# Key stage of a hybrid decoder step: prompt compression interleaved with the first sample's keys, compressed scores computed per sample, first score units moved behind the loop

## The chip, the cores and the metric

The program runs on one core of one Trainium2 chip. The metric is the device time of one execution in microseconds (us); lower is better. The engines' names in the profile: PE is TensorE (PEld its weight loads), DVE is VectorE, ACT is ScalarE, POOL is GpSimd, SP is SyncE, which in this kernel only issues transfers.

## The reference, cut to what matters

One layer of a decoder for 512 prompt tokens and 8 samples with 2048 past tokens each. Two groups of heads share one input projection: stick-breaking attention (`sb`, 8 heads) and NSA (8 query heads on 2 key heads) with a compressed, a selected and a window branch. For the samples, keys and values lie in caches by pages of 128 tokens (16 pages for each sample). The part that the change touches computes for every sample:

```python
z = einsum('bqhd,bshd->bhqs', q, k) / sqrt(64)            # stick-breaking scores of all 2048 cached keys
kc = silu((blocks_k + pe_k) @ w_ck1) @ w_ck2               # compressed keys: blocks of 32 tokens, stride 16
vc = silu((blocks_v + pe_v) @ w_cv1) @ w_cv2               # the same for values: 127 blocks a sample, 31 for the prompt
s_c = einsum('bkgqd,bkcd->bkgqc', qg, kc) * scale          # compressed scores
s_s = einsum('bkgqd,bkqnld->bkgqnl', qg, kg) * scale       # scores of the selected pages; the window's likewise
```

`pe @ w1` is the same for all blocks; the kernel adds it as a bias (`pebias`), for one column per hidden unit.

## The kernel before, in words

Each engine has a program of its own, written out by hand; semaphores order them. There is no scheduler: what stands in a row in the code of an engine is issued in that row, and an instruction that waits holds up all behind it on its engine. The stages in order of time: norm and input projection (to about 182 us), transposes of queries and keys (182 to 189), the key stage (189 to 454), the two attention stages for the prompt with the samples' small steps and value pages among them, the output projection and the MLP.

**Ahead of the loop of the key stage (before).** PE multiplies `pe` by `w1`, one column at a time (two times 16 products, lines 745 to 750), DVE copies the two columns to `pebias` (L1729, L1730). Then `compress(0, 1, ...)` compresses the prompt's own keys and values: PE transposes (`chunks_T`, L780), multiplies by `w1` (`hidden`, L794: four groups of 8 products, two for keys, two for values), ACT copies the transposes (L1308) and makes the sigmoid (`sigmoid`, L1312), DVE finishes the silu (`silu`, L1734, L1742), PE multiplies by `w2`. POOL reorders tokens ahead of each (`permute`, L2202, L2205). All else of the key stage waits until this is done.

**The loop (before).** Four turns of two samples. For one sample:
- SP (`load_keys`, L525) issues 50 transfers: the sample's stick-breaking query row (L529), 2 times 8 pieces of the *next* sample's tokens to be compressed (`load_chunks`, L495, L498), the selection keys in quads of 4 pages (L540), 16 pages of stick-breaking keys into a ring of 8 slots (L543), the window keys as a fifth quad (L546). A quad waits until PE has transposed the quad two before it, a ring slot until DVE has reduced the page before it in the slot. Page numbers come by a table load (L491), four times a sample.
- PE (`compress(c, 2, between)`, L774) does the same work as for the prompt with 127 blocks. In six places it calls `between()`, which takes the next piece of key work: `keys_T` (L756, four transposes of a quad, waits for the quad) or `key_scores` (L765). Pieces: T0; S0 and T1; S1 and T2; S2 and T3; S3 and T4; S4. Pieces five and six stand ahead of the `w2` products.
- DVE takes pages of the ring (`sb_keys`, L1752: a product L1760, a sum L1764): 8 pages, the silu of the keys, 6 pages, the silu of the values, 2 pages, two copies (`compressed_out`, L1745).

**Behind the loop (before).** All compressed scores (8 small products), the gates (one product), ACT rounds five constant masks to fp32r (L1370, L1374; the last two wait for the compressed scores), takes a softplus over 1024 columns (L1378, L1379) and only then the first unit of the stick-breaking stage, `sb_ln(0)` (L1387 to L1389). PE issues `sb_qk(0)`, the first unit's scores, behind the gates. DVE prepares the samples' scores (L1984 to L1996), waits for the transposed row maxima (`row_max_diagonal`, L1816, L1817) and then takes `sb_soft(0)` (L2006). A unit of this stage runs PE, ACT, DVE, ACT, DVE, PE, ACT in a chain.

## Time and profile before

| | us |
|---|---|
| median of 3 runs | 1187.35 (1182.03 to 1191.99) |
| the profiled execution | 1191.54 |
| its span | 1189.7 |
| mean granted TensorE clock | 0.929 of full |
| PE busy | 1084.4 (91%) |
| DVE, ACT, POOL busy | 617.1, 392.6, 69.9 |

The profile is of one execution, whose time was 1191.54 us, 4.2 us above the median of the runs; 1.8 us of it lie outside its span. Times in the timeline are us from the span's start. A row of the timeline merges instructions of one kind that follow each other; fp32 products show as two instructions each, so a `key_scores` of 4 products is 8 in the rows. PE's busy time counts a product from its start to its modelled end, whatever the clock; the granted clock stands in rows of its own (1.00 is 2.4 GHz, 0.50 is 1.2 GHz).

### The profile page before, as it was taken

The numbers are of one execution on the slowest core, as the hardware profiler recorded it, in microseconds if no ns is written. First come the engines' busy times: TensorE is split into PE (matmuls) and PEld (weight loads), VectorE is DVE, ScalarE is ACT, GpSimd is POOL, SyncE is SP. The second block draws the span as 40 slices with busy tenths as digits, with TensorE's granted clock in tenths as the row PEclk, the third lists the DMA queues.
The fourth block names the chain that finished last, engine by engine and source line by source line (L and its number), as shares of the span: only waits on it lengthen the run. The fifth ranks groups of instructions, "written<-read, shape, count | busy, mean of one in ns | idle before, by whom it ended". The sixth has DMA issues, their size and how long they took to land.

```text
span 1189.7 us, 23077 instructions
## 1 busy us (share of the span) xinstructions
PE 1084.4 (91%) x8348; PEld 953.0 (80%) x8348; DVE 617.1 (52%) x1042; ACT 392.6 (33%) x725; POOL 69.9 (6%) x83
## 2 busy tenths in 40 slices
PE   3996999998989998989999898999999999999993
PEld 2996999887878886555555557999999999999993
DVE  4431673586778787765444436445543335553332
ACT  4120212333333335556444435332231112221223
POOL 2000001221112100000000000110000000000002
PEclk9998997798999896988999978999999999999997
DMA  7529218799999963256666651323333333332321
GB/s 248 178 79 222 79 40 230 188 241 246 268 265 275 273 209 115 90 187 202 212 200 205 212 177 36 89 71 88 88 106 89 94 85 89 94 97 72 90 71 72
DMA packets 180131, 177.61 MB, mean 149 GB/s; under 512 B 13063, under 2 KB 140676, under 8 KB 177700
## 3 DMA queue, kind: packets, MB, share of 16 engines
q1 hardware_dynamic: 178610, 171.33, 50.7%
q10 hardware_dynamic: 1458, 5.43, 1.4%
q8 instruction: 40, 0.66, 0.2%
q14 instruction: 23, 0.19, 0.1%
HBM read 170.83 MB, written 10.06 MB: 152 GB/s over the span
## 4 chain that ended last, share of the span: by engine, by line
PE 64%; SPq 18%; issue 6%; DMA 4%; DVE 3%; ACT 3%; POOL 0%; POOLq 0%; DVEq 0%; ACTq 0%
PE bank L662 59%; SPq L576 4%; PE bank L666 4%; SPq L498 3%; SPq L540 2%; SPq L564 2%; SPq L543 2%; SPq L491 2%; DMA low_arena<-in_cache_nsa_slc_kv_dram 1%; DMA low_arena<-in_consts_dram 1%; DMA high_arena<-in_cache_sb_kv_dram 1%; DMA high_arena<-in_w_in_dram 1%; ACT low_arena L1550 1%; SPq L504 0%; SPq L582 0%
## 5 line engine op out<-in xcount | busy, mean ns | idle before, releaser
L662 PE MATMUL bank<-high_arena 128*128 128x254 f32 (+8 forms) x1864 | 239.6, 346 | 16.5 <-DMA high_arena<-in_cache_sb_kv_dram 6.6
L662 PEld LDWEIGHTS bank<-high_arena 128*128 128x128 f32 (+5 forms) x1864 | 185.2, 152 | 53.6 <-issue 10.1
L2114 DVE TENSOR_TENSOR w_low<-high_arena,w_high 128x1024 fp32r<-128x1024 f32 x72 | 90.1, 1252 | 84.1 <-ACT w_high L1487 74.2
L666 PE MATMUL bank<-low_arena 128*128 128x128 f32 (+3 forms) x658 | 108.0, 309 | 28.0 <-DMA page_ids<-in_page_table_dram 14.7
L666 PEld LDWEIGHTS bank<-low_arena 128*128 128x128 f32 (+3 forms) x658 | 87.4, 164 | 39.6 <-issue 27.2
L1487 ACT ACTIVATE w_high<-high_arena 128x1024 fp32r<-128x1024 f32 x72 | 76.3, 1060 | 114.8 <-PE bank L662 113.8
L662 PE MATMUL bank<-a_high,w_high 128*128 128x256 f32 (+1 forms) x512 | 104.3, 285 | 5.3 <-issue 2.9
L662 PE MATMUL bank<-h_high,w_high 128*128 128x256 f32 (+1 forms) x512 | 103.1, 283 | 1.8 <-DVE h_low L2141 1.8
L662 PE MATMUL bank<-a_low,w_high 128*128 128x256 f32 (+1 forms) x512 | 103.8, 284 | 0.0
L662 PE MATMUL bank<-a_high,w_low 128*128 128x256 f32 (+1 forms) x512 | 103.5, 283 | 0.0
L662 PE MATMUL bank<-h_low,w_high 128*128 128x256 f32 (+1 forms) x512 | 103.3, 283 | 0.0
L662 PE MATMUL bank<-h_high,w_low 128*128 128x256 f32 (+1 forms) x512 | 103.2, 283 | 0.0
L1764 DVE TENSOR_REDUCE low_arena<-low_arena 128x512 f32 x128 | 87.9, 686 | 18.3 <-DVE low_arena L1760 0.6
L662 PE MATMUL bank<-w_in_high,h_high 128*128 128x284 f32 x320 | 96.1, 300 | 0.8 <-issue 0.8
L662 PE MATMUL bank<-w_in_low,h_high 128*128 128x284 f32 x320 | 94.7, 296 | 0.0
L662 PE MATMUL bank<-w_in_high,h_low_in 128*128 128x284 f32 x320 | 94.6, 296 | 0.0
L1760 DVE TENSOR_TENSOR low_arena<-low_arena,high_arena 128x512 f32<-128x512 f32 x120 | 86.1, 718 | 12.0 <-DMA low_arena<-in_cache_sb_kv_dram 11.9
L662 PEld LDWEIGHTS bank<-a_high,w_high 128*128 128x128 f32 x512 | 80.0, 190 | 6.1 <-issue 5.9
L662 PEld LDWEIGHTS bank<-h_high,w_high 128*128 128x128 f32 x512 | 79.4, 188 | 2.0 <-issue 2.0
L662 PEld LDWEIGHTS bank<-a_high,w_low 128*128 128x128 f32 x512 | 80.0, 190 | 0.0
L662 PEld LDWEIGHTS bank<-a_low,w_high 128*128 128x128 f32 x512 | 79.9, 189 | 0.0
L662 PEld LDWEIGHTS bank<-h_high,w_low 128*128 128x128 f32 x512 | 79.6, 189 | 0.0
(218 smaller groups left out, 1583.6 us busy)
## 6 DMA issues: line engine op xcount, KB each, us to landing
low_arena<-in_cache_sb_kv_dram SPq DMA_DIRECT2D x128, 256.0 KB, 4.9
high_arena<-in_cache_sb_kv_dram SPq DMA_DIRECT2D x128, 256.0 KB, 3.7
high_arena<-in_cache_nsa_cmp_kv_dram SPq DMA_DIRECT2D x128, 128.0 KB, 5.2
high_arena<-in_w_up_dram SPq DMA_DIRECT2D x32, 512.0 KB, 4.1
high_arena<-in_w_down_dram SPq DMA_DIRECT2D x32, 512.0 KB, 4.2
high_arena<-in_w_in_dram SPq DMA_DIRECT2D x10, 1136.0 KB, 5.6
low_arena<-in_cache_nsa_slc_kv_dram SPq DMA_DIRECT2D x128, 64.0 KB
high_arena<-in_cache_nsa_slc_kv_dram SPq DMA_DIRECT2D x128, 64.0 KB, 2.4
```

The lines of the kernel that those rows point to most:

```text
L491: return nc.values_load_multi_w_load_instructions(pt[0:1, ds(lo, 8)], engines=[mybir.EngineType.SP], min_val=0, max_val=NPHYS - 1, skip_ru ...
L498: sp.dma_start(nat[u][half][16 * p:16 * p + 16].rearrange("p t k h d -> p (t k h d)"), c_cmp[ds(pg, 1)].rearrange("o (c t) k h d -> (o c) ...
L540: sp.dma_start(kquad[n % 2][:, j], c_slc[ds(pages[p + j], 1), :, 0].rearrange("o s h d -> (o s) (h d)")).then_inc(sem(f"kq_in{n % 2}"), 16)
L543: sp.dma_start(kring[p], c_sb[ds(pages[p], 1), :, 0].rearrange("o s h d -> (o s) (h d)")).then_inc(sem(f"ring_in{p}"), 16)
L564: sp.dma_start(ring[:, u, :], c_sb[ds(pages[u], 1), :, 1].rearrange("o s h d -> (o s) (h d)")).then_inc(sem(f"ring_in{u}"), 16)
L576: sp.dma_start(quad[:, q, j, :], c_slc[ds(pages[4 * (q % 2) + j], 1), :, 1].rearrange("o s h d -> (o s) (h d)")).then_inc(sem(f"quad_in{q} ...
L662: return T.matmul(out, lhsT=l, rhs=r, start=start, stop=stop, **k)
L666: return T.transpose(out, in_, ident[0:n, 0:n])
L1487: S.activation(w_hi_r[u], w_raw[u], ACT.Copy).then_inc(sem(f"w_hi{u}"), 1)
L1760: chain(V.tensor_tensor(k, k, qb[:, u, :], ALU.mult))
L1764: V.tensor_reduce(raw_scores(ds(i, 1), u)[:, p, :], k.rearrange("p (h d) -> p h d", h=H), AX.X, ALU.add).then_inc(sem(f"ring_free{p % 8}"), 1)
L2114: V.tensor_tensor(w_lo_r[u], w_raw[u], w_hi[u], ALU.subtract).then_inc(sem(f"w_lo{u}"), 1)
```

## The change

1. **Loads.** The compression tokens of sample 1 are loaded behind the last weight block of the input projection, in place of in the key stage (`load_keys(0, 0, False)`). SP no longer waits for `snew` ahead of all key loads, only ahead of ring slot 7. The buffers `nat[1]`, and that of the prompt's tokens, lie elsewhere.
2. **Bias.** The 32 one-column products go. The prompt's `hidden` takes 66 columns for 62: two more per key head, of which one comes out as `pe @ w1`. DVE copies it from there (`bias`).
3. **Front.** Three pieces of sample 0's key work (T0; S0 and T1; S1 and T2) stand inside the prompt's `compress`, and DVE takes pages 0 to 6 of sample 0 among the prompt's silus. Samples 0 and 1 are written out, the loop has three turns.
4. **Compressed scores.** Each sample's 8 columns are computed within its `compress`, behind the `w2` product of the keys, and copied by ACT with the other scores (`csc`). DVE copies the compressed keys ahead of the silu of the values. PE's piece five stands behind the keys' `w2` product.
5. **Early.** The gates' product and ACT's rounding of all five masks stand in and behind sample 0.
6. **Behind the loop.** PE issues `sb_qk(0)` and `sb_qk(1)` first; ACT takes `sb_ln(0)` ahead of the softplus.

```diff
@@ SP @@
             load_columns(*COLUMNS[1])
+            sp.wait_ge(sem("z_mm"), 5 * NCB // 2)
+            for half in range(2):
+                load_chunks(page_ids(NPG + 8 * half), 1, half)
...
+                        if p == 7:
+                            sp.wait_ge(sem("snew"), 2)
                         sp.wait_ge(sem(f"ring_free{p}"), i * 4 + 2 * u + half + 1)
...
             sp.wait_ge(sem("sbq_out"), 16)
-            sp.wait_ge(sem("snew"), 2)
-
-            with sp.Fori(0, 3) as i:
+
+            load_keys(0, 0, False)
+            load_keys(0, 1, True)
+            with sp.Fori(1, 3) as i:
                 for u in range(2):
                     load_keys(i, u, True)
@@ PE @@
             pe.wait_ge(sem("cmpw_in"), 64)
-            for kv in range(2):
-                for m in range(16):
-                    ins = mm(bank[6][:, kv:kv + 1], w1[kv][:, m, :], vcol[:, 24 + 16 * kv + m:25 + 16 * kv + m],
-                             m == 0, m == 15)
-            ins.then_inc(sem("start_pe"), 1)
...
+                nh = nb if tiles == 2 else NCP + 2
...
-                        mm(out, w1[kv][:, m, :], xT[kv][:, m, :, 0:nb], m == 0, False)
-                        ins = mm(out, w1[kv][:, 8 + m, :], xT[kv][:, m, :, 1:nb + 1], False, m == 7)
+                        mm(out, w1[kv][:, m, :], xT[kv][:, m, :, 0:nh], m == 0, False)
+                        ins = mm(out, w1[kv][:, 8 + m, :], xT[kv][:, m, :, 1:nh + 1], False, m == 7)
...
                 hidden(1, 1)
-                between()
-                between()
                 pe.wait_ge(sem("hid_ready0"), c + past + 1 + 1)
...
                 ins.then_inc(sem("w2_mm0"), 1)
+                between()
+                if past:
+                    pe.wait_ge(sem("kvc_ev0"), c + past + 1 + 1)
+                    mm(bank[7][0:NC, 160:160 + H], kc[:, 0, 0:NC],
+                       qbd[:, ds(c, 1), :].rearrange("p o j -> p (o j)"))
+                between()
...
-            compress(0, 1, lambda: None)
-            with pe.Fori(0, 4) as i:
+            todo = key_work(0, 0)
+            compress(0, 1, next_of(todo, 3))
+            todo[2:2] = [lambda: None, sample_gates, lambda: None]
+            compress(0, 2, next_of(todo))
+            compress(1, 2, next_of(key_work(0, 1)))
+            with pe.Fori(1, 4) as i:
...
-            sample_scores()
-            sample_gates()
-            pe.wait_ge(sem("masks_in"), 1)
...
+            pe.wait_ge(sem("masks_in"), 1)
+            sb_qk(0)
+            sb_qk(1)
+            for kv in range(2):
+                pe.wait_ge(sem(f"kvc_ev{kv}"), B + 1 + 1)
+            pe.wait_ge(sem("qs_ev"), B + 1)
@@ ACT @@
+            todo = key_copies(0, 0)
+            compress(0, 1, lambda: todo.pop(0)() if len(todo) > 1 else None)
+            sample_keys(0, 0, todo)
+            act.wait_ge(sem("sbq_out"), 16)
+            act.wait_ge(*signal("g_mm", 1))
+            for dst, name in ((ident_r, "ident"), (causal_r, "causal"), (before_r, "before"), (ntri_r, "ntri"), (nones_r, "nones")):
+                ins = S.activation(dst, K(name), ACT.Copy)
+            ins.then_inc(sem("masks_in"), 1)
...
                 if s < SB_U:
                     sb_ln(s)
+                if s == 0:
+                    sample_softplus()
@@ DVE @@
+            def bias(kv):
+                dve.wait_ge(sem(f"hid_mm{kv}"), 1)
+                col = bank[2 + kv][:, NCP + 1:NCP + 2]
+                chain(V.tensor_copy(pebias[:, kv:kv + 1], col))
+                V.tensor_scalar(pebias[:, 2 + kv:3 + kv], col, -1.0, None, ALU.mult).then_inc(sem("start_dve"), 1)
...
+            def sample_work(i, u, begun=0):
+
+                c = i * 2 + u
+                sb_keys(i, u, begun, 8)
+                silu(c, 0, NCH)
+                sb_keys(i, u, 8, 14)
+                keys_compressed(c, kc[:, 0, 0:NC], NCH)
+                silu(c, 1, NCH)
+                sb_keys(i, u, 14, 16)
+                values_compressed(c, vc[0:NC, ds(c, 1), :].rearrange("p o c -> p (o c)"), NCH)
+
+            sb_keys(0, 0, 0, 2)
+            bias(0)
+            sb_keys(0, 0, 2, 4)
             silu(0, 0, NCP + 1)
+            sb_keys(0, 0, 4, 5)
+            bias(1)
+            sb_keys(0, 0, 5, 7)
             silu(0, 1, NCP + 1)
```

PE between the last transpose of the queries and the second group of the prompt's products; a product with 62 or 66 columns is one of `hidden`, 128x64 a transpose of the prompt's tokens, 128x128 with a wait on `kq_in` a key quad (T), 128x8 key scores (S). Before:

```order
L662 MATMUL bank<-low_arena_49,high_arena_50 128x1 [waits cmpw_in]
L662 MATMUL bank<-low_arena_49,high_arena_50 128x1 x31
L666 MATMUL bank<-low_arena_49 128x64 [waits start_dve,perm,qkT_ev0,xT_ev0,qkT_ev1]
L666 MATMUL bank<-low_arena_49 128x64 x3
L666 MATMUL bank<-low_arena_49 128x64 [waits xT_ev0,perm]
L666 MATMUL bank<-low_arena_49 128x64 x3
L662 MATMUL bank<-high_arena_50 128x62 [waits xT_ev0,hid_ready0]
L662 MATMUL bank<-high_arena_50 128x62 x7
```

And now:

```order
L677 MATMUL bank<-low_arena_49 128x64 [waits start_dve,qkT_ev0,perm,qkT_ev1,xT_ev0,cmpw_in]
L677 MATMUL bank<-low_arena_49 128x64 x3
L677 MATMUL bank<-low_arena_49 128x128 [waits kq_ev,kq_in0]
L677 MATMUL bank<-low_arena_49 128x128 x3
L677 MATMUL bank<-low_arena_49 128x64 [waits xT_ev0,perm]
L677 MATMUL bank<-low_arena_49 128x64 x3
L673 MATMUL bank<-high_arena_50 128x66 [waits xT_ev0,hid_ready0]
L673 MATMUL bank<-high_arena_50 128x66 x7
L673 MATMUL bank<-high_arena_50 128x8 [waits qs_ev,kq_ev]
L673 MATMUL bank<-high_arena_50 128x8 x3
L677 MATMUL bank<-low_arena_49 128x128 [waits kq_ev,kq_in1]
```

The one-column products are gone, and the second instruction group of the prompt's compression now stands behind a wait for the first key quad.

DVE at the end of the prompt's compression and in sample 0 now (L1788 and L1792 are a page's product and sum, L1757 and L1758 the bias, L1769 a silu):

```order
L1757 COPY high_arena<-bank 128x1 [waits hid_mm1]
L1758 TENSOR_SCALAR high_arena<-bank 128x1 [waits dve_steps]
L1788 TENSOR_TENSOR low_arena<-low_arena,high_arena 128x512 [waits ring_in5]
L1792 TENSOR_REDUCE low_arena<-low_arena 128x8 [waits dve_steps]
L1788 TENSOR_TENSOR low_arena<-low_arena,high_arena 128x512 [waits ring_in6]
L1792 TENSOR_REDUCE low_arena<-low_arena 128x8 [waits dve_steps]
L1769 SCALAR_TENSOR_TENSOR high_arena<-bank,high_arena 128x2x31 [waits w2_mm1,hid_e1]
L1774 COPY high_arena<-bank 128x31 [waits w2_mm0]
L1778 COPY high_arena<-bank 31x128 [waits w2_mm1]
L1788 TENSOR_TENSOR low_arena<-low_arena,high_arena 128x512 [waits ring_in7]
L1792 TENSOR_REDUCE low_arena<-low_arena 128x8 [waits dve_steps]
L1769 SCALAR_TENSOR_TENSOR high_arena<-bank,high_arena 128x2x127 [waits w2_mm0,hid_e0]
```

Two pages stand between the values' bias and the values' silu of the prompt, and page 8 still stands behind the keys' silu of sample 0 (the last row).

PE behind the loop, before (`before_r,ident_r` is the mask product of a unit; 127x8 the compressed scores):

```order
L662 MATMUL bank<-high_arena_50 127x8 [waits qs_ev,kvc_ev1,kvc_ev0]
L662 MATMUL bank<-high_arena_50 127x8 x7
L662 MATMUL bank<-high_arena_50,low_arena_49 128x192 [waits rows_in]
L662 MATMUL bank<-low_arena_49 128x128 [waits masks_in]
L662 MATMUL bank<-low_arena_49 128x128
L662 MATMUL bank<-before_r_64,ident_r_60 128x128 x2
L666 MATMUL bank<-low_arena_49 64x128 [waits samples_dve]
L662 MATMUL bank<-low_arena_49 128x256 x2
```

And now:

```order
L673 MATMUL bank<-low_arena_49 128x128 [waits masks_in]
L673 MATMUL bank<-low_arena_49 128x128
L673 MATMUL bank<-before_r_64,ident_r_60 128x128 x2
L673 MATMUL bank<-low_arena_49 128x256 x2
L673 MATMUL bank<-before_r_64,ident_r_60 128x128 x2
L677 MATMUL bank<-low_arena_49 64x128 [waits qs_ev,samples_dve,kvc_ev1,kvc_ev0]
```

Two units' scores come first; the transpose of the row maxima (64x128) stands behind them.

## Rows read from the trace of the kernel before

**Rows 1.** The page, part 2: busy and clock in 40 slices of 29.7 us.
```profile
PE   3996999998989998989999898999999999999993
...
PEclk9998997798999896988999978999999999999997
```
**Rows 2.** Busy time by stretch, one per sample: us, PE, PEld, DVE, ACT, POOL, clock, DMA, GB/s.
```profile
369.46:396.00 26.54, 25.52 (x167) 23.21 (x166) 22.79 (x38) 10.17 (x21) 6.01 (x8) 0.98 1.02 261
...
sum 234.90, PE 217.37 PEld 196.66 DVE 179.75 ACT 82.98 POOL 39.15; mean PE 27.17 PEld 24.58 DVE 22.47 ACT 10.37 POOL 4.89
```
**Rows 3.** What SP's queue waited for, 185 to 460 us: total, times, longest.
```profile
SPq L540 <- PE bank L666: 16.1, 8, 6.9
...
SPq L551 <- DVE high_arena L1721: 4.3, 1, 4.3
```
**Rows 4.** Timeline of SP's queue, start us and us: query rows, first chunks, ring loads.
```profile
194.12 0.37 SPq L529 DMA_DIRECT2D high_arena<-sb_queries  x1
195.46 4.03 SPq L498 DMA_DIRECT2D high_arena<-in_cache_nsa_cmp_kv_dram  x8
...
235.30 0.34 SPq L529 DMA_DIRECT2D high_arena<-sb_queries  x1
...
249.37 1.88 SPq L543 DMA_DIRECT2D low_arena<-in_cache_sb_kv_dram  x4
...
414.12 0.43 SPq L529 DMA_DIRECT2D high_arena<-sb_queries  x1
```
**Rows 5.** Busy time by stretches of 2 us (columns as in rows 2).
```profile
190.00:192.00 2.00, 2.00 (x20) 2.00 (x20) 1.90 (x4) 1.59 (x2) 2.00 (x4) 1.00 1.04 426
...
216.00:218.00 2.00, 1.71 (x11) 1.46 (x10) 0.00 (x0) 0.58 (x2) 0.00 (x0) 0.50 0.96 148
```
**Rows 6.** The query rows' transfers (L529), from issue to landing.
```profile
DMA to landing us min/median/max: 4.6/6.6/8.2
```
**Rows 7.** Timeline of PE, 188 to 245 us.
```profile
189.39 9.94 PE L662 MATMUL bank<-low_arena,high_arena 128*128 128x1 f32 x64
...
206.04 3.67 PE L662 MATMUL bank<-high_arena 128*128 128x62 f32 x16
...
218.73 0.64 PE L662 MATMUL bank<-high_arena 128*31 128x64 f32 x4 [1.02 <-DVE high_arena L1742]
219.30 3.68 PE L666 MATMUL bank<-low_arena 128*128 128x128 f32 x16
...
229.16 3.59 PE L662 MATMUL bank<-high_arena 128*128 128x254 f32 x16
...
240.10 4.38 PE L662 MATMUL bank<-high_arena 128*128 128x254 f32 x24
```
**Rows 8.** Timeline of DVE: the prompt's last silu, then sample 0.
```profile
218.40 0.28 DVE L1742 SCALAR_TENSOR_TENSOR high_arena<-bank,high_arena 128x62 f32<-128x62 f32 x1 [7.16 <-ACT high_arena L1319]
...
234.28 0.48 DVE L1742 SCALAR_TENSOR_TENSOR high_arena<-bank,high_arena 128x254 f32<-128x254 f32 x1 [2.57 <-ACT high_arena L1319]
234.68 0.68 DVE L1760 TENSOR_TENSOR low_arena<-low_arena,high_arena 128x512 f32<-128x512 f32 x1
...
236.11 0.82 DVE L1760 TENSOR_TENSOR low_arena<-low_arena,high_arena 128x512 f32<-128x512 f32 x1
...
245.22 0.48 DVE L1742 SCALAR_TENSOR_TENSOR high_arena<-bank,high_arena 128x254 f32<-128x254 f32 x1 [1.34 <-ACT high_arena L1319]
```
**Rows 9.** Timeline behind the loop: PE, ACT, DVE.
```profile
455.01 3.55 PE L662 MATMUL bank<-high_arena 128*127 128x8 f32 x16 [0.84 <-DVE high_arena L1748]
...
459.16 0.39 DVE L1996 COPY high_arena<-high_arena 64x31 f32<-64x31 f32 x2
...
461.09 0.28 DVE L1816 TENSOR_REDUCE low_arena<-bank 64x1 f32<-64x128 f32 x1 [1.55 <-PE bank L666]
461.14 0.36 ACT L1387 ACTIVATE high_arena<-bank 128x256 f32<-128x256 f32 x1
...
462.53 0.42 DVE L2006 SCALAR_TENSOR_TENSOR high_arena<-bank,high_arena 128x256 f32<-128x256 f32 x1 [0.87 <-ACT high_arena L1389]
```

More of the change, by code:

```diff
@@ L194, with __init__ @@
 class Turns:
-    def __init__(self, chain, count, per):
-        self.chain, self.count, self.per = chain, count, per
+    def __init__(self, chain, count, per, start=0):
+        self.chain, self.count, self.per, self.start = chain, count, per, start
     def __enter__(self):
@@ L202, in __enter__ @@
         self.first = c.n
-        self.loop = c.eng.Fori(0, self.count)
+        c.n = self.base = c.n - self.start * self.per
+        self.loop = c.eng.Fori(self.start, self.start + self.count)
         i = self.loop.__enter__()
@@ L1696, in _ @@
             V.memset(st[0:1, 204:205], 0.0).then_inc(sem("start_dve"), 1)
+            for kv in range(2):
+                ins = V.tensor_copy(xT[kv][:, :, :, NCP + 1:NCP + 3],
+                                    over(vcol[:, 24 + 16 * kv:40 + 16 * kv].rearrange("p (two m) -> p m two", two=2), 2, KVH))
+            ins.then_inc(sem("start_dve"), 1)
             for j in range(0, 14, 2):
```

162 lines of the change are left out of this document (75 added, 87 removed).

## The prediction

> **What bounds the kernel now.** I read the page's slices first: PE is busy nearly all of the span and its clock is granted in full, but for a few slices; two of the low ones are the seventh and eighth, 178 to 238 us, where the key stage begins [rows 1]. The change works there and up to the end of that stage, so I then cut the stage by sample. The eight samples take 234.9 us. The cheapest is the sixth with 26.5 us at a clock of 0.98, while the mean is 29.4, so PE's own work is not the whole price [rows 2]. SP's queue tells the rest: in the whole stage it waited 16.1 us for PE in 8 places, the longest 6.9, and by the timeline these lie before 235 and behind 414; between its query rows at 235.30 and 414.12 it issues without a pause, 178.8 us for six samples or 29.8 each [rows 3, 4]. From sample 1 on the stage goes at SP's pace. So a change of the front pays only as far as it brings SP sooner to its unbroken run, and behind the loop only as far as it brings the first stick-breaking unit sooner.
>
> **Part 1: where SP stands.** SP's wait for `snew` ended at 194.1 after 4.3 us; without it SP starts at 189.8 [rows 3, 4]. Without 16 chunk transfers (two groups like that of 4.03 us) and their page numbers it also has some 10 us less to issue. Taken alone that is 14 us (I come back to it as a rival). The chunks go where SP and the transfer engines have room, behind the last weight block: cost nothing; if they held up that block, PE would wait by up to their 8 us, but they stand behind it in the same queue.
>
> The run starts, however, when ring slots come free, and these come from DVE, which waits for PE. So I follow that loop.
>
> *First key quad.* Query row at 189.8, page numbers as before 1.34 us (194.12 to 195.46), then four transfers of 0.5 us: the last goes out at 192.6 [rows 4]. The engines have just then finished the prompt's stores: their share is 1.04 at 190 to 192 [rows 5]. A landing takes 4.6 to 8.2 us for 256 KB, as much as a quad; the queue is empty, so 4.6: 197.2 [rows 6]. Bounds: 3 us sooner or 3.6 later.
>
> The Trainium skill, DMA: Bandwidth & Descriptors, on the anatomy of one DMA, gives about 2.0 us of fixed cost and the bytes on top. By it the quad would land 1 to 2 us sooner and the time would be as much lower. No row shows a landing under 4.6 for this size, so it gives the forecast nothing.
>
> *The prompt's compression.* The one-column products filled 189.39 to 199.33 [rows 7]; they go, 9.9 us. But now PE stands from about 191.5 to 197.2 in front of the quad. From there its work until the values' `hidden` is done, at the price of the half clock, goes by its kinds of groups. H, eight products, 3.67 (206.04; 66 columns for 62 cost at most 0.2 more each), four times: 14.7. T, four transposes, 3.68/4 = 0.92, three times: 2.8. S, four key scores, half of the 3.55 of the eight compressed scores, 1.78, twice: 3.6. Two small transposes of the prompt, 0.6 each: 1.2 [rows 7, 9]. Sum 22.3; with 0.5 for hand-overs it ends at 220.0 (before 217.7, as ACT's sigmoid and DVE's silu ended at 218.7). The first half, which ends the keys' `hidden`, is 12.2: 209.4. Then DVE: bias 0.2, two pages of 1.43 (234.68 to 236.11), 2.9, and as before 0.9 from the silu to PE's first transpose of sample 0 (218.40 to 219.30) [rows 7, 8]. Sample 0 starts at 224.0: **4.7 later** than now.
>
> Why the half clock: before, from 194 on, one-column and 62-column products ran at 0.50, and still did at 216 to 218 with PE busy 1.71 of 2 us [rows 5]. The new front has the same products and an idle stretch in front of them.
>
> *Sample 0.* To the end of the keys' `hidden` PE had T0; S0, T1 beside the rest and took 13.4 us (219.3 to 232.7). Now it has S2, T3; S3, T4: one S more at half clock, +1.8. So DVE's silu, before at 234.28, comes 4.7 + 1.8 = 6.5 later and page 8, which stands behind it, starts at 241.2 for 234.68. Six pages 8.6 and the silu 0.4, then pages 14 and 15, 2.9: slot 7 is free at 253.1 (the values' `hidden` has three pieces fewer and is done in time) [rows 7, 8]. SP's load into slot 7 was issued last of the four of 249.37, at 250.8, and nothing held it but SP [rows 4]. **+2.3 us** for the start of SP's unbroken run, and the 29.8 us per sample behind it stay: all that is issued is the same. Bounds: the rivals below, -9 and +6.
>
> **Part 2: in the loop.** One compressed score of 0.2 (3.55/8 at half clock is 0.44; at full clock half) per sample is added, and the keys' `w2` product of 0.3 moves into a place where PE waited 0.8 for ACT's copy of the last quad. DVE's copy of 0.3 ahead of the values' silu falls into its idle 1.34 [rows 8]. ACT copies 0.2 more. Under SP's pace all of it is hidden; for the last sample, which goes at PE's pace, -0.3 at best: I take **-0.2**, bounds -0.5 and +0.5 each for the one or two samples at PE's pace. The five mask copies, 1.0 us on ACT once between samples 0 and 1, may cost 0.5; DVE, not PE, is last there, so 0. The gates' product, 1 us, lies in sample 0 before the values' `hidden`, which has slack: 0.
>
> **Part 3: behind the loop.** Eight scores (3.55) and the gates (1.0) go from PE's path, the masks and the softplus (2.2) from ACT's. ACT could start the first unit 5.5 us sooner than 461.14. But DVE is late next: its preparation ends at 459.5 whatever PE does (459.16 and two copies of 0.2), less the 0.2 copy of the compressed scores. Then, as between 461.09 and 461.7, the diagonal, 0.6: `sb_soft(0)` starts at 460.1 for 462.53 [rows 9]. **-2.4 us**, and from there on the chain of a unit is as it was. What stands ahead of ACT's rounding of the unit, the softplus, waits for DVE until 457.3 and ends at 459.5, in time. Bounds: -1 (softplus or row maxima late) and -4.4 (everything removed pays).
>
> **Sum.** +2.3 - 0.2 - 2.4 = -0.3 us against the profiled execution (1191.54, span 1189.7). That execution is 4.2 above the median of the runs, so I set the sum against the median: 1187.35 - 0.3 = **1187.0**. A measurement of this kernel tells about 1% (12 us) from no change.
>
> **Rivals.**
> 1. *The clock comes up inside the prompt's compression.* For it: with T and S among them PE has denser work from 197 on. Then four H are 7.4 for 14.7, T and S half. The second and third quad become the limit (issued 0.47 us a transfer, landing 201.5 and 207), the values' `hidden` ends at 211, sample 0 starts at 215.4, the silu comes at 229, slot 7 is free at 241.5: -9.3, with the rest -12: **1175**. Against: [rows 5] show 0.50 for work as dense as that, 190s to 220s. The Trainium skill, TensorE: Matmul & The Clock Gate, on the HAM clock gate, says that sustained activity releases the throttle; by that rule a PE that works without a stop from 197 on would get its full clock back there, and this rival would be the case. The trace before does not agree: busy over 0.85 and still 0.50.
> 2. *SP keeps its whole lead.* 14 us and 2.6 behind: **1171**. For it: 14 us are really gone from its queue. Against: slots 0 to 7 wait for pages 8 to 15, and page 8 stands behind a silu that waits for PE.
> 3. *Slower: the key quads land late.* They now stand in PE's path in the prompt's compression, each behind ring loads in the one queue. At the longest landing, 8.2 us [rows 6], the first comes 3.6 later, and the window quad of sample 0, issued only when page 7 has freed its slot (226), lands at 235, when PE wants it. With 1 to 2 us for that, and low clock again behind it: +6 and up: **1193**. It decides from a landing of 6 us on, since PE has no other work ahead of T0.
> 4. *The change doesn't do what it says:* ACT's first unit isn't sooner since DVE's steps hold all. Then part 3 is -0.5, 1189; it lies in the forecast's own range.
>
> **Chances.** Forecast with rival 4, 1182 to 1191: 0.58. Rival 1 in full or in part: 0.20. Rival 2: 0.10. Rival 3: 0.12. The range takes in rival 3 and rival 1: 1173 to 1193. Faster by over 1% (below 1175.5): rival 2 (0.10), most of rival 1 (0.13), and 0.03 of the forecast's case for a stage that gives more than I see: 0.26. Slower by over 1% needs twice the price of rival 3: 0.08. Within 1%: 0.66.
>
> **What would show it right or wrong.** In the new trace: PE idle from about 191.5 to 197 in front of a key transpose; granted clock 0.50 to beyond 220; the prompt's last silu near 223 and sample 0's first transposes near 224; page 8 near 241; SP pausing some 6 us in front of the first ring load of sample 1, and then six samples of 29.8 us. The loop's end some 2 us later than 454.2, and `sb_soft(0)` 5.9 us behind the last `w2` product for 8.4 now. The forecast is wrong if the clock is 1.00 between 200 and 215, if page 8 starts before 235, or if the samples behind the front take less than 29 us each.

## The result, and the profile after

The changed kernel takes 1196.25 us in the median of 20 runs (1184.91 to 1206.91), the kernel before 1185.28 in 20 (1178.09 to 1195.18): a ratio of 1.0092, with a 95% interval of 1.0066 to 1.0118. It is some 11 us slower, where 1187.0 and "no change" had been forecast. The profiled execution took 1196.56 us (span 1194.7). The interval leaves out 1.000, so the loss is real, though smaller than the scatter of single runs. The ratios, here and below, leave out runs over 1.5% above the fastest of their kernel: two of the 20 here, and four of the twelve of e1 below, whose median over all twelve is 1.0097 of that of the kernel before.

The page's slices, which answer to [rows 1]:

```profile
PE   3997997898978998888998988999999999999993
...
PEclk9998996698888888799999898999999999999996
```

The seventh and eighth slice have 6 for 7, and slices 10 to 15, in the loop, have 8 six times, where four of them had 9 before. By sample (columns as in [rows 2]):

```profile
220.04:249.72 29.68, 26.89 (x141) 23.57 (x141) 12.18 (x21) 8.71 (x19) 4.85 (x8) 0.87 0.60 143
...
311.33:339.76 28.43, 27.77 (x167) 25.20 (x168) 22.18 (x36) 10.42 (x21) 5.41 (x8) 0.91 0.89 234
339.76:376.09 36.33, 27.08 (x168) 24.28 (x168) 23.20 (x37) 10.55 (x24) 5.62 (x8) 0.91 1.07 235
...
406.82:441.82 35.00, 30.91 (x169) 27.44 (x168) 23.55 (x38) 10.91 (x25) 5.56 (x8) 0.82 0.85 233
...
sum 249.96, PE 224.82 PEld 200.97 DVE 172.32 ACT 83.63 POOL 37.54; mean PE 28.10 PEld 25.12 DVE 21.54 ACT 10.45 POOL 4.69
```

The eight samples take 249.96 us for 234.90. The fifth alone takes 36.33, of which PE is busy 27.08: it stood for 9. PE is busy 7.5 us more over all, at a lower clock. So the stage from sample 0 on lost 15 us, and the forecast had -0.2 in the loop. The fifth and the seventh sample of the kernel before, for comparison:

```profile
338.68:369.46 30.78, 26.69 (x167) 24.07 (x166) 22.30 (x37) 10.38 (x21) 5.59 (x8) 0.94 1.06 272
...
396.00:426.44 30.44, 27.75 (x165) 25.04 (x166) 22.62 (x37) 10.48 (x21) 5.48 (x8) 0.89 0.95 265
```

Comparing moments needs one care. What lies ahead of the key stage scatters by some us from execution to execution (the prompt's first store goes out at 175.00 us here, at 178.27 in the trace before, and between 174.97 and 181.70 in the eighteen kernels tried below), so I count from that store, and call it S. Four places carry the ledger:

| | before | after | difference |
|---|---|---|---|
| sample 0's first transposes, behind S | 41.0 | 45.0 | +4.0 |
| SP loads sample 1's second page into slot 7, behind S | 72.7 | 76.2 | +3.5 |
| DVE's last copy of compressed values, behind S | 276.4 | 295.7 | +19.3 |
| from there to `sb_soft(0)` | 7.90 | 5.73 | -2.2 |

The front and the end are about as forecast; between the second row and the third 15.8 us are lost. At `sb_soft(0)` the changed kernel is 17.1 us behind; at the end of the span it is 8.3 behind, counted from S. Between 520 and 720 us, in stages whose code is the same, the granted clock was 0.97 for 0.88 in the trace before, which gives back most of that; it is one execution against one, and I read nothing of the change into it.

What did SP do in the loop? The chain of waits of the changed kernel at the end of sample 3, followed back through SP (start us, us, what):

```profile
330.23 0.45 SPq L556
330.67 0.04 issue
330.72 0.04 SPq L564
330.75 0.04 issue
330.80 0.05 SPq L564
330.85 3.92 issue
334.77 0.04 SPq L564
```

L564 is the end of `with sp.Fori(1, 3)`: a register is counted up, a branch is taken at 330.80, and the next instruction comes 3.92 us later. "issue" means that SP waited for nothing that the profile shows. The same place of the kernel before:

```profile
326.15 0.45 SPq L546
326.59 0.04 issue
326.64 0.03 SPq L553
326.67 0.04 issue
326.71 0.04 SPq L553
326.76 0.23 issue
326.98 0.04 SPq L553
```

There the branch cost 0.23 us (and 0.27 at 265.9, where the loop turned the first time). What the gap does, 5 us on, in the timeline of PE and DVE:

```profile
341.28 1.92 SPq L548 DMA_DIRECT2D low_arena<-in_cache_nsa_slc_kv_dram  x4
...
347.24 1.96 PE L677 MATMUL bank<-low_arena 128*128 128x128 f32 x8 [6.43 <-DMA low_arena<-in_cache_nsa_slc_kv_dram]
347.82 0.69 DVE L1788 TENSOR_TENSOR low_arena<-low_arena,high_arena 128x512 f32<-128x512 f32 x1 [6.98 <-DMA low_arena<-in_cache_sb_kv_dram]
```

The quad and the page of the ring are issued late; PE stands 6.43 us for the one and DVE 6.98 us for the other. By SP's query rows sample 3 lasts 35.9 us for 30.2, and 3.7 of these 5.7 us are the gap. From sample 4, the fifth, on PE then works at a lower clock: granted 0.91, 0.89, 0.82 and 0.92 for 0.94, 0.98, 0.89 and 0.93 before. From these figures I estimate some 30 us at half clock for some 15, and PE is busy 113.9 us for 106.9 in these four samples, with the same products but for one compressed score each. That fits a standing which comes back as a slower PE, and in sample 6 SP waits for PE (1.7 us in front of its window quad). It is one trace against one, and no run takes apart how much of the stage's 15.8 us each of these steps carries. SP's longest wait for PE, 5.5 us at 427.1, is another matter: it lies in sample 7, where SP runs ahead of PE in every kernel (3.5 us at the same place before).

The page's third part has the trace of it in one line, the queue that loads instructions (packets, MB, share). Before, and after:

```profile
q14 instruction: 23, 0.19, 0.1%
```
```profile
q14 instruction: 33, 0.27, 0.1%
```

Ten more loads of 8 KB each. Not all of them belong to the gap: the changed kernel with its loop moved (e13 and e17 below) has no gap and still 28 and 29 loads, so that four or five of the ten go with the branch and the rest stay without it. What ties the gap to a load is its time. By the trace's records one begins at 333.15 us, within the gap, and has ended 1.3 us before SP's next instruction; in the kernel before no load lies behind either branch.

### The profile page after: what moved, and what is told of

The parts are those of the page before. It is cut to its first block, busy times and chain, and to the rows that moved or that the text cites. A ratio compares the mean times of both kernels' runs of the same rounds, so it can differ in the third digit from the quotient of the medians.

```text
span 1194.7 us, 22803 instructions
## 1 busy us (share of the span) xinstructions
PE 1071.5 (90%) x8284; PEld 941.7 (79%) x8284; DVE 619.2 (52%) x1045; ACT 394.5 (33%) x733; POOL 69.0 (6%) x83
## 4 chain that ended last, share of the span: by engine, by line
PE 58%; SPq 18%; issue 7%; DVE 7%; DMA 5%; ACT 4%; POOL 0%; ACTq 0%; POOLq 0%; DVEq 0%
PE bank L673 54%; SPq L587 4%; PE bank L677 4%; SPq L503 3%; SPq L548 3%; SPq L553 2%; SPq L575 2%; SPq L496 2%; DMA high_arena<-in_w_in_dram 2%; DMA low_arena<-in_cache_nsa_slc_kv_dram 1%; DMA low_arena<-in_consts_dram 1%; DVE w_in_low L1656 1%; ACT low_arena L1570 1%; DMA high_arena<-in_cache_sb_kv_dram 0%; SPq L509 0%
## 5 line engine op out<-in xcount | busy, mean ns | idle before, releaser
L673 PE MATMUL bank<-high_arena 128*128 128x254 f32 (+8 forms) x1864 | 244.8, 345 | 21.1 <-DMA high_arena<-in_cache_sb_kv_dram 9.9
L673 PEld LDWEIGHTS bank<-high_arena 128*128 128x128 f32 (+4 forms) x1864 | 190.1, 155 | 58.9 <-issue 15.5
L1788 DVE TENSOR_TENSOR low_arena<-low_arena,high_arena 128x512 f32<-128x512 f32 x120 | 86.8, 723 | 22.6 <-DMA low_arena<-in_cache_sb_kv_dram 22.6
L1792 DVE TENSOR_REDUCE low_arena<-low_arena 128x512 f32 (+1 forms) x128 | 87.8, 686 | 14.8 <-DVE low_arena L1788 0.5
```

The costliest lines, as they stand in the source:

```text
L673: return T.matmul(out, lhsT=l, rhs=r, start=start, stop=stop, **k)
L1788: chain(V.tensor_tensor(k, k, qb[:, u, :], ALU.mult))
L1792: V.tensor_reduce(raw_scores(ds(i, 1), u)[:, p, :], k.rearrange("p (h d) -> p h d", h=H), AX.X, ALU.add).then_inc(sem(f"ring_free{p % 8}"), 1)
```

## The experiments

All ratios are to the kernel before, with their 95% intervals.

### SP or the engines?

Four kernels tell "SP's list" (theory A) from "PE's and DVE's order" (theory B).

**e1_wait_once**, the changed kernel with

```
-                        if p == 7:
+                        if p == 7 and half == 0 and isinstance(i, int) and i * 2 + u == 0:
                             sp.wait_ge(sem("snew"), 2)
```

> 

> The changed kernel, but SP's wait for `snew` in front of ring slot 7 is issued for sample 0's first half alone, and no longer twice a sample. Theory A (the key stage goes at the pace of SP's instructions, so that whatever SP gains or loses between two query rows stays in the time): two instructions less per sample, 0.4 us by the query rows (29.69 between 335.04 and 364.73 in the changed kernel, 29.29 for the same sample before), some 2.5 us over seven samples; and the 3.9 us that SP stands behind its loop's branch (330.85 to 334.77) may go or stay, since the loop's code gets shorter by four instructions. Together 2 to 7 us less than the changed kernel, ratio to before 1.003 to 1.008. Theory B (the loss comes from PE and DVE: the compressed score and the copy of the compressed keys stand between PE's products and DVE's pages): no change, 1.009.

Measured 1.0065 (1.0030 to 1.0101), 3.83 us behind the branch. The two instructions take 0.05 us each in SP's row, not 0.4 together. DVE's last copy came 295.8 us behind S for 295.7: the wait carries nothing that can be seen in the trace. The time can't decide it, since the interval reaches from a third of the loss to all of it.

**e2_written_out**, the changed kernel with

```
-            with sp.Fori(1, 3) as i:
+            for i in range(1, 3):
```

> 

> The changed kernel, but SP's loop over samples 2 to 5 is written out, sample by sample, with no branch and with constants for the waits' values. Theory A: the 3.9 us behind the branch go, and a written-out sample costs SP about 28.8 us for 29.7 (as sample 6 before, 28.4 between query rows, for 29.25): 4 x 0.9. In all 7 us less than the changed kernel, ratio to before 1.003; the query rows of samples 2 to 7 are at most 30 us apart and no gap in SP's row is over 1 us without a wait. Theory B: no change, 1.009, since PE and DVE go on at their own pace.

Measured 0.9997 (0.9973 to 1.0021). The loss is gone, with all that the change does to PE, ACT and DVE in place. Query rows of samples 2 to 7 are 28.6 to 29.9 us apart (after: 29.7 to 35.9). This speaks for A and leaves B no room.

**e3_before_written_out**, the same edit in the kernel before, `for i in range(3)`.

> 

> The kernel before, but SP's loop over samples 0 to 5 is written out. Theory A: four or five samples of 28.4 for 29.8 us, 4 to 6 us less: ratio 0.995 to 0.997, the loop ends near 449 for 454.2 behind the same start. Theory B: the same time, 1.000, because SP isn't what bounds. A third reading, that code which runs once must be fetched and costs more than code in a loop: slower, 1.003 and up, with gaps in SP's row at instruction loads.

Measured 0.9998 (0.9968 to 1.0027). Theory A's gain of 4 to 6 us isn't there: the interval allows 3.8 at most. So writing out is worth nothing by itself in a kernel whose branch is cheap; what e2 took away was something that only the changed kernel has.

**e4_scores_behind**, the changed kernel with its compressed scores behind the loop again (in the loop):

```
                 hidden(1, 1)
+                between()
+                between()
...
                 ins.then_inc(sem("w2_mm0"), 1)
-                between()
-                if past:
...
-                between()
```

and DVE's and ACT's copies put back to match.

> 

> The changed kernel with one part undone: the compressed scores are computed behind the loop again, by eight products and a copy of DVE's, and in the loop the keys' `w2` product, DVE's copy of the compressed keys and ACT's copies stand as before; SP's list is untouched. Theory A: in the loop nothing changes, behind it 1 us is lost at most (the products stand behind the first two units' scores): ratio 1.009 to 1.010, and the 3.9 us behind SP's branch are there again. Theory B: the samples go back to 29.4 us, 8 to 12 us less: ratio 0.999 to 1.002.

Measured 1.0102 (1.0063 to 1.0140), 4.58 us behind the branch. Theory B had 0.999 to 1.002: it falls, for what the change does in the loop.

### Is it the branch?

**e6_before_loop_of_two**, the kernel before, nothing of the change in it but the loop's shape:

```
-            with sp.Fori(0, 3) as i:
+            for u in range(2):
+                load_keys(0, u, True)
+            with sp.Fori(1, 3) as i:
                 for u in range(2):
                     load_keys(i, u, True)
```

> 

> The kernel before, with one edit: SP's samples 0 and 1 are written out and its loop runs over turns 1 and 2, as in the changed kernel; what is issued, and in which order, is as before. Theory A1 (a loop of which nothing but this shape has changed has to fetch its first instructions again at its branch): some 4 us between the branch near 327 and the next instruction, and the time 4 to 9 us longer than before: ratio 1.003 to 1.008. Theory A2 (it isn't the shape but something else of the change that makes the branch slow): 0.3 us behind the branch, ratio 1.000.

Measured 1.0067 (1.0031 to 1.0103). The chain of waits of this kernel at its branch:

```profile
323.64 0.05 SPq L555
323.69 4.53 issue
328.22 0.04 SPq L555
```

This is the study's plainest run: the same transfers in the same order, and most of the loss.

**e7_code_shifted**, the changed kernel with 64 superfluous waits in SP's list far ahead (two of them become one instruction, so the loop moves by 32 places and not by the 64 of the expectation):

> 

> The changed kernel with 64 superfluous waits (already met) in SP's list far ahead, behind the norm, in a stretch where SP waits anyway: the loop is the same, but its instructions stand 64 places further on in the program. Theory P (what counts is where the loop's code stands with respect to the blocks of 8 KB in which it is fetched): the gap behind the branch changes, possibly to 0.3 us, and the ratio falls to 1.001 to 1.004. Theory S (the loop is too long for what is kept, wherever it stands): 3.8 to 4.6 us as before, ratio 1.009.

Measured 1.0107 (1.0067 to 1.0148), 4.74 us behind the branch. By itself it spoke for theory S (the loop is too long wherever it stands); it was the wrong shift, as the next kernels show.

**e5_delay_4us** and **e8_written_out_wait_once** are e2 with one thing more each: seven loads of page numbers meant as a delay, and the wait for `snew` issued once.

> 

> The changed kernel with SP's samples written out (as e2, ratio 0.9997), and seven superfluous loads of eight page numbers (0.53 to 0.57 us each, some 4 us) in SP's list in front of sample 4's query row, where the changed kernel stands 3.9 us behind its branch. Theory A (the key stage goes at SP's pace, and the standing behind the branch is the main loss): SP's query rows from sample 4 on come 4 us later and stay so; the next key quad comes 4 us later, PE stands for it some 6 us, the granted clock falls behind that, and the whole run is 4 to 9 us longer than e2: ratio 1.003 to 1.008. Theory C (the standing is absorbed by what lies ready in the ring, and e2 gained by its quicker samples alone): ratio 1.000 as e2.

> 

> The changed kernel with SP's samples written out and the wait for `snew` issued once: the best version that the study has in view. Theory A: two instructions less per sample (0.1 to 0.4 us) than e2, so 1 to 2.5 us less than e2's 0.9997 of before: ratio 0.998. Theory B or C: as e2, 1.000. That it beats the kernel before by more than the interval (0.3%) isn't expected of either.

Measured 1.0028 (1.0000 to 1.0056) and 0.9991 (0.9956 to 1.0026). In e5 the trace has one load of page numbers where eight were written: what nobody used had been dropped, the delay that was to be tested isn't there, and the run repeats e2. That two runs of one program gave 0.9997 and 1.0028 is a measure of how far to trust the last digit.

### Shape or place?

Counting SP's instructions in the traces, the loop's first one comes 300 places later in e6 than before, and 304 later in the changed kernel. The next two kernels shift code with waits that are already met, in a stretch where SP stands for the rope anyway. e9 is e6 with 168 of them, e10 the kernel before with 128:

```
+            for _ in range(168):
+                sp.wait_ge(sem("h_ready"), 2)
             sp.wait_ge(sem("rope_done"), T5)
```

> 

> As e6 (the kernel before with SP's samples 0 and 1 written out and a loop of two turns, which stood 4.53 us behind its branch and took 1.0067), with 168 superfluous waits, 84 instructions, in SP's list where it waits for the rope anyway. By the trace's count the loop's first instruction came 300 places later in e6 than before; with 84 more it is 384, three times 128, and 128 instructions of 64 bytes are the 8 KB of one instruction load. Theory P (what counts is how the loop lies in these blocks): the gap behind the branch is 0.3 us as before, and the time falls by most of what e6 lost: 1.000 to 1.002. Theory R (what counts is how much has been run since the last branch, 344 instructions before, 644 in e6, 728 here): 4 to 5 us again, 1.007.

Measured 0.9998 (0.9963 to 1.0032). Its chain at the branch:

```profile
327.65 0.05 SPq L557
327.70 0.25 issue
327.95 0.04 SPq L557
```

> 

> The kernel before, its loop of three turns untouched, with 128 superfluous waits (64 instructions, half a block) in SP's list where it waits for the rope anyway. Theory P: the loop now lies across one block more, SP stands some 4 us behind each of its two backward branches, near 266 and 327, and the time is 1.007 to 1.015 of before. Theory R: 408 instructions since the last branch for 344; if the bound lies between 408 and 644, nothing changes, 0.3 us and 1.000.

Measured 1.0140 (1.0090 to 1.0190), the largest effect of the study, from waits that wait for nothing. At its two branches:

```profile
264.75 0.05 SPq L555
264.80 3.32 issue
268.12 0.04 SPq L555
...
329.01 0.05 SPq L555
329.06 5.52 issue
334.58 0.04 SPq L555
```

The two together settle it: theory P (what counts is where the loop lies in the blocks of code) holds, theory R (how much has run since the last branch) falls. e6's loss goes when its loop is moved on by 84 places, and the kernel before gets the loss when its own is moved by 64.

The price of standing alone, from the kernel before with its samples written out and 128 met waits in front of sample 4:

> 

> The price of a standing SP by itself: the kernel before with its samples written out (e3, 0.9998) and 64 superfluous wait instructions, 3.9 us at the 0.061 us that one took in e7, in front of sample 4's query row. In e5 the same was meant, but the loads put there had been dropped from the program, which makes e5 a repetition of e2. Theory A: query rows from sample 4 on 4 us later to the end, the loop's end 4 us later or more, since PE stands and its granted clock falls: 1.003 to 1.008. Theory C (what lies ready absorbs it): 1.000.

Measured 1.0048 (1.0015 to 1.0080); from sample 3's window load at 326.24 to sample 4's query row 4.81 us pass, for 1.08 before. Against e3 (0.9998) that is 0.5% or 6 us for 3.7 us more of standing, to be held against the branch's own 0.67% (e6) and 1.4% for two (e10). The intervals are too wide to say that a gap by loading costs more than one by waits.

The fourth kernel goes after a better version. It is e2, and all key work of sample 0 stands behind the prompt's compression:

```
-            compress(0, 1, next_of(todo, 3))
-            todo[2:2] = [lambda: None, sample_gates, lambda: None]
+            last = todo.pop()
+            todo.append(lambda: (last(), sample_gates()))
+            compress(0, 1, lambda: None)
             compress(0, 2, next_of(todo))
```

with ACT's and DVE's order to match.

> 

> The changed kernel with SP's samples written out (e2), and the key work of sample 0 taken out of the prompt's compression: PE computes that at once instead of standing 3.9 us for the first key quad. Expected by the prediction's own reckoning of the front: the prompt's compression needs four groups H, 14.7 us, and its small parts, so it is done near 207 for 216; sample 0 starts near 210 for 220.0, and page 8, which sets slot 0 free, comes at 226 to 230 for 237.6. If SP's place counts from there on as in rival 2, its unbroken run starts 8 to 11 us sooner, the loop ends as much sooner, unless PE's own 27 us a sample bound then: 4 to 11 us less than e2, ratio 0.990 to 0.996. If what SP gains is lost again to waits for slots: 1.000 as e2.

Measured 0.9951 (0.9912 to 0.9989): faster than both kernels. Its PE in the front:

```profile
200.32 0.66 PE L677 MATMUL bank<-low_arena 64*128 64x64 f32 x4 [6.42 <-ACT high_arena L1318]
200.91 3.68 PE L673 MATMUL bank<-high_arena 128*128 128x66 f32 x16
...
218.97 3.68 PE L677 MATMUL bank<-low_arena 128*128 128x128 f32 x16
```

Sample 0 starts 38.6 us behind S (before 41.0, after 45.0), not the 35 that I had expected: PE stands 6.42 us for ACT's copy of the prompt's chunks, and its first products of 66 columns start 20.6 us behind S in both (200.91 here, 195.56 in the changed kernel). So the 3.92 us that the changed kernel stood for its first quad had cost nothing. That the gain is what the key work took inside the prompt's compression at half clock is argued and not shown: sample 0 starts 6.4 us sooner than in the changed kernel, but in this trace DVE's last copy comes 277.5 us behind S, for 277.1 in e2's.

### The changed kernel, its loop moved back

Met waits at the place that e9 and e10 used, in the changed kernel: 160 of them in e13, 128 in e15, 208 in e16.

> 

> The changed kernel itself, its loop of two turns kept, with 160 superfluous waits (80 instructions) in SP's list where it waits for the rope anyway. The loop's first instruction came 304 places later than in the kernel before; now it is 384, three times 128, so that it lies in the blocks of 8 KB as before. Theory P (the cause of the loss is the branch's instruction load, nothing that the change does): 0.3 us behind the branch, samples of 29 to 30 us, ratio 0.998 to 1.002, as with the loop written out. If the loss has another cause in the changed kernel beside it: 1.004 and up with the gap gone.

> 

> One look at the changed kernel, its loop moved by 64 instructions: 368 places behind that of the kernel before, which is 112 of a block of 128. So far the gap behind the branch was short at 0 and 4 us long at 44, 45, 48, 64 and 80. If what counts is that the loop of 336 instructions touches three blocks and not four, at most 48 neighbouring places are good ones; 112 is one of them if 0 lies at least 16 places behind the first. Either 0.3 us or 4 us, and no theory of mine says which; it bounds the good places on one side.

> 

> One look at the changed kernel, its loop moved by 104 instructions: 408 places behind that of the kernel before, which is 24 of a block of 128. It bounds the good places on the other side: if at most 48 neighbouring places are good and 0 is among them, then of 112 and 24 at least one and perhaps both have 0.3 us behind the branch. If both have 4 us the good places are fewer than 40.

e13 measured 1.0048 (1.0014 to 1.0083) with 0.25 us behind the branch:

```profile
333.55 0.05 SPq L566
333.60 0.25 issue
333.85 0.04 SPq L566
```

e15, a single run of 1184.52 us, has 0.26 us behind the branch; e16, a single run of 1191.78 us, has 4.90. Since e13 lay between the theories it was run again, and once with the wait for `snew` taken out of the loop.

> 

> e13 once more, the changed kernel with its loop moved back to its old place within a block (1.0048, 1.0014 to 1.0083). Its interval leaves out both that the standing behind the branch is the whole loss (1.000) and that it is none of it (1.009). If it is the whole: 0.998 to 1.002, and e13 was high by scatter. If about half is left, from the later start of SP's run (ring slot 7 of sample 1 is loaded 76.7 us behind the prompt's store for 72.7 in the kernel before): 1.003 to 1.006.

> 

> As e17, and the wait for `snew` issued once (166 superfluous waits, 83 instructions, so that the loop of 332 instructions begins at the same place within a block). If the waits in the loop carry part of what is left, 0.4 us a sample by the query rows of the changed kernel: 2 to 3 us less than e17, 0.998 to 1.003. If they cost the 0.05 us each that stand in SP's row: as e17 within 1 us.

Measured 1.0003 (0.9975 to 1.0032) and 1.0012 (0.9977 to 1.0048). e13 and e17 are one program, and their mean is 1.0026: most of the loss goes with the gap, and whether some 3 us of it stay is open. The waits in the loop cost nothing that shows.

> 

> As e12 (the changed kernel, SP's samples written out, the prompt's compression ahead of sample 0's key work: 0.9951), and the wait for `snew` issued once. Expected: as e12 within the interval, 0.993 to 0.997, with two instructions of 0.05 us less per sample; it also repeats e12, whose profiled execution (span 1184.0) didn't show the gain that its median did. If e12's gain was scatter: 0.998 to 1.000.

Measured 0.9962 (0.9929 to 0.9995): the gain of e12 holds, and here DVE's last copy comes 272.8 us behind S.

All runs with a loop in one table. The place counts SP's instructions from the kernel before's first one of the loop, and what is left of it in a block of 128 (why 128, is said below); the loads are those of the page's q14 line:

| kernel | loop begins | in a block | us behind each turn's branch | loads |
|---|---|---|---|---|
| before | 0 | 0 | 0.27, 0.23 | 23 |
| e10 | 64 | 64 | 3.32, 5.52 | 34 |
| e6 | 300 | 44 | 4.53 | 31 |
| e9 | 384 | 0 | 0.25 | 26 |
| e1 | 301 | 45 | 3.83 | 33 |
| changed, e4 | 304 | 48 | 3.92, 4.58 | 33, 33 |
| e7 | 336 | 80 | 4.74 | 33 |
| e15 | 368 | 112 | 0.26 | 29 |
| e13, e17 | 384 | 0 | 0.25, 0.25 | 28, 29 |
| e18 | 384 | 0 | 0.25 | 28 |
| e16 | 408 | 24 | 4.90 | 33 |

The loop has 332 to 336 instructions, 2.6 blocks. Started at 112 or 0 of a block it turns for 0.23 to 0.27 us; at 24, 44, 45, 48, 64 and 80 it stands for 3.3 to 5.5 and loads 4 to 6 blocks more a turn. In each of the eight long gaps a load of 8 KB lies inside, and SP goes on 1.3 to 1.5 us behind its end; behind none of the seven short ones does a load begin within 3 us. In the stage, too, the two kinds are apart: DVE's last copy of compressed values comes 286.4 to 296.4 us behind S in the seven kernels with a long gap, and 272.2 to 284.5 in the twelve that have neither a long gap nor e11's delay. The places fit a loop which must touch three blocks and not four: then at most 48 of the 128 places are good, and 112 to 0 lie among them. Where exactly they begin and end wasn't tried. The Trainium skill, Runtime: NRT & Kernel Launch, on instruction fetch mechanics, says that a taken branch whose target is outside what the engine holds has to fetch it before it goes on; the runs agree, with 3.3 to 5.5 us for it. The same section gives refills of 16 KB, 256 instructions, with two held; by that size of an instruction a load of 8 KB, as all of this queue are here, is 128. Counted in 256 the good places would be 0, 112 and 128 with bad ones on both sides between them (44 to 80, and 152 for e16), which one stretch of good places can't give; counted in 128 they lie side by side. The measurement decides for 128, if the good places are one stretch.

## Why the prediction was wrong

That the stage goes at the pace of SP's list from sample 1 on was read rightly for the kernel before, but for two short waits: of SP's eight waits for PE, two of 0.7 us together lie between 300 and 410, not before 235 or behind 414. What failed is a step of part 1, in its own words: "the 29.8 us per sample behind it stay: all that is issued is the same". All that is issued was the same, but the loop around it wasn't: the diff makes `Fori(0, 3)` a `Fori(1, 3)` with two samples written out ahead, which moves the loop by 304 instructions. The branch back then cost 3.92 us for 0.23, in just the queue that the prediction had named as the bound, with no slack to take it. The term should have read: 3.7 us more of standing, priced at 6 to 8 us by e11 and e6, with PE's lower clock behind it. The step from that price to the changed kernel's whole loss of 11 us lies within the intervals.

Point by point:

- *Part 1, the front.* Counted from S, sample 0 started 4.0 us later (forecast 4.7), page 8 6.2 later (62.6 for 56.4; forecast 6.5), SP's run 3.5 later (forecast 2.3). DVE's rows of the changed kernel:

```profile
219.15 0.27 DVE L1769 SCALAR_TENSOR_TENSOR high_arena<-bank,high_arena 128x62 f32<-128x62 f32 x1
...
237.17 0.48 DVE L1769 SCALAR_TENSOR_TENSOR high_arena<-bank,high_arena 128x254 f32<-128x254 f32 x1 [15.42 <-ACT high_arena L1330]
237.56 0.72 DVE L1788 TENSOR_TENSOR low_arena<-low_arena,high_arena 128x512 f32<-128x512 f32 x1
```

  and SP paused 8.3 us in front of sample 1's first ring load (forecast some 6):

```profile
SPq L553 <- DVE low_arena L1792: 28.1, 9, 8.3
SPq L548 <- PE bank L677: 10.6, 5, 5.5
```

- *The half clock* to beyond 220, over rival 1: right. PE's rows from 196 to 222 (columns as in [rows 2]):

```profile
196.00:206.00 10.00, 10.00 (x50) 9.55 (x49) 0.89 (x2) 1.03 (x3) 2.34 (x4) 0.50 0.64 193
206.00:216.00 10.00, 10.00 (x49) 9.55 (x48) 4.36 (x9) 1.89 (x5) 2.72 (x4) 0.50 0.35 105
216.00:222.00 6.00, 3.09 (x19) 2.66 (x19) 4.73 (x11) 1.51 (x4) 0.00 (x0) 0.50 0.26 87
```

  PE was busy 20 of 20 us and was granted 0.50 all the while.
- *PE stands for the first quad.* Forecast 191.5 to 197; in the trace 3.92 us up to 192.48. The quad's last transfer was issued at 189.41, so it landed within 3.1 us, for the 4.6 that the prediction took from [rows 6]. That no landing of 256 KB is under 4.6 was wrong of the trace before, too, where the ring's pages of that size took 3.0 to 8.6 (L543). The prediction's figure from the Trainium skill, DMA: Bandwidth & Descriptors, on the anatomy of one DMA, is given there for transfers issued by GpSimd; these are SP's, and they did land 1.5 us sooner, as it said. The time didn't come down by that, since the standing cost nothing, as e12 showed.
- *Part 2, the work added in the loop.* By e4 against the changed kernel (1.0102 and 1.0092) it costs or gives nothing that can be measured: right as to the engines, and the wait for `snew` (e1, e18) too.
- *Part 3, behind the loop.* -2.2 us for -2.4. The end of the chain:

```profile
469.97 0.64 PE L673 MATMUL bank<-low_arena 64*128 64x128 f32 x4
...
475.44 0.39 DVE L2036 COPY high_arena<-high_arena 64x31 f32<-64x31 f32 x2
475.91 0.28 DVE L1858 TENSOR_REDUCE low_arena<-bank 64x1 f32<-64x128 f32 x1
...
476.39 0.41 DVE L2046 SCALAR_TENSOR_TENSOR high_arena<-bank,high_arena 128x256 f32<-128x256 f32 x1
```

  DVE's preparation is last, as said: ACT had the unit's scores ready at 472.7, and `sb_soft(0)` stands behind the diagonal in [rows 9]'s order.
- *The sum.* Six kernels keep the change and don't stand behind a branch: e2, e5, e8, e13, e17, e18, at 0.9997, 1.0028, 0.9991, 1.0048, 1.0003 and 1.0012. Their mean is 1.0013, with some 0.0013 to either side if the runs are taken as independent (some share their runs of the kernel before): +1.5 us where the prediction's sum was -0.3. The three that are written out have 1.0005 in the mean, the three with the loop kept and moved 1.0021. So the branch carries 0.7 to 0.9 of the 0.92%. Of the 1.8 us between +1.5 and -0.3, SP's start has 1.2; the interval, 1.5 us to either side, can't tell the rest from nothing. That the rest of the sum came out so near is in part luck: nothing here is measured to better than 1.5 us.
- *Rival 3* had the right sign for the wrong place: the key quads that came late were not those of the front but those behind the branch, 6.43 us at 347.24. The signs of being wrong named samples of less than 29 us, and none of more than 30.

## What to carry to other kernels

A queue that bounds a stage is bounded by its instructions too, the branch and its code included: if an edit peels turns off a loop or puts instructions ahead of it, look in the chain of waits for an "issue" of some us behind the loop's last line, before looking for a cause in what was edited. SP's loop of 332 to 336 instructions turned in 0.23 to 0.27 us or in 3.3 to 5.5, by where it happened to begin; writing it out or moving it cured that, and a comparison of two versions is worth little until both are on the same side. And work that moves into a stretch at half clock takes nearly twice as long there: in the changed kernel eight products of 128x8 took 1.72 us at 221.80, with 0.50 granted, and 0.96 at 255.92, with 1.00. Computing the prompt's part alone and first was the one order that beat both kernels.

## What the runs showed of the hardware

- Behind a taken branch with an instruction load of 8 KB in its gap SP stood 3.3 to 5.5 us (seven kernels, eight branches); with none, 0.23 to 0.27 (six kernels, seven branches).
- Moving code by waits that are already met changed the whole kernel's time by up to 1.4% (e10), more than the change under study.
- Two met waits in a row share an instruction, and in a row of such instructions each takes 0.061 us (e7, e9, e10, e11).
- A standing of 4 us in the queue that bounds cost 6 us of the whole (e11, 1.8 to 9.5 by its interval). In the changed kernel PE stood longer than SP did, 6.43 us, and that sample and the two behind it went at a granted clock of 0.91, 0.89 and 0.82, for 0.94, 0.98 and 0.89 before.
- PE worked without a pause from 196 to 216, on products of 66 columns and transposes, and was granted 0.50 all the while.
